# Feed-forward of a two-block transformer: a third quad of weight tiles in seven products, with its late sums made by accumulating DMAs

## The chip, the core and the metric

The kernel runs on one core of a Trainium2 chip, as one launch. The metric is the device time of one execution in microseconds (us), the median of several. The engines that matter here are PE (TensorE, the matrix products), DVE (VectorE), ACT (ScalarE), POOL (GpSimd, which here only issues DMAs) and SP (SyncE, whose queue issues the loads of the weights).

## What is computed

Two transformer blocks over 256 tokens of width 2048 in float32. The part that the change touches is the gate and up projection of the first block's feed-forward, with D = 2048 and D_FF = 5632:

```python
h = rms_norm(x, norm_ffn[l])
x = x + (jax.nn.silu(h @ w_ffn_gate[l]) * (h @ w_ffn_up[l])) @ w_ffn_down[l]
```

## The kernel before, in words

**Tiles.** A weight tile is 128 rows by 512 columns (256 KB). The 256 tokens are two halves j of 128. The kernel works through some 400 chunks of four tiles (1 MB); chunk g lies in slot g % 4 of `raw`, and SP issues its load as soon as the chunk four before it has been read for the last time.

**Splitting.** Each tile goes through PE three times, because both operands are split into a rounded high part and a low part. For each *piece* (mostly two tiles) ACT writes `whi` = high part of `raw` (`piece_hi`, L427), DVE writes `wlo` = `raw` - `whi` (`piece_lo`, L432), and PE runs for each product the three matmuls of `three` (L2610 to L2612): high x high, high x low, low x high, each over 512 columns. `whi` and `wlo` have SPLITS = 4 slots: ACT may start on piece q only when PE is done with piece q - 4 (`wait_ge(mm_done, q - (SPLITS - 1))`).

**The phases.** D_FF is 11 blocks f of 512 columns. Block 0 is phase "ffn", block 10 is "ffz", and the nine blocks f = 1 to 9 (NSUM = 9) are phase "ffs", which the change is about. A block of "ffs" has eight *quads* (`pos` = 0 to 7), one chunk each: two tiles of the gate weight and the two tiles of the up weight at the same rows. A quad is a 2 x 2 product of blocks (two token halves by gate and up, summed over two tiles of rows). Done plainly (`eight_products`) it has eight products, so 24 matmuls, in two pieces of 12. By Strassen's scheme in Winograd's form (`seven_products`) it has seven, so 21 matmuls, in four pieces: n = 0 with 6 matmuls (two raw tiles), n = 1 with 3 (one tile), n = 2 with 6 and n = 3 with 6, the last two on *sums* of weight tiles. Before, positions 3 and 5 are such quads (`SEVEN = {3: 0, 5: 1}`). Of their sums DVE makes all: one addition over two tiles (L438), and then two over one tile each (L440, L442), all between pieces n = 1 and n = 2 (`block_sums`). The sums and differences of the activations (`SH`, `SL`) are made once, in phase "ffn".

**The banks.** A block sums into four of the eight banks of PSUM (`own_banks`), and its seven-product quads also into the other four (`shared_banks`), which are the own banks of the block before. After the last seven-product quad ACT copies one shared bank (`FO`, L1285) and DVE combines them (`fold_shared`, L466 to L471, four operations); PE starts the next block only after that (`wait_ge(fold, ...)`). At `pos` 1 of the next block DVE adds the folded values to the own banks of the block before (`summed`, L1878 to L1881), which frees them; the first seven-product quad of a block waits for this on PE. ACT then does the silu (`silu_summed`, L1253, after `pos` 2), DVE multiplies and transposes (`gated_sum`, L1887 and L1861, after `pos` 2), and 16 small DMAs that SP issues between its weight loads (`turn_block`, at c = 5, 6, 7) turn the block, which is split after `pos` 6 (`gated_hi`, `gated_lo`).

**Order.** Every engine runs one list of instructions written out by hand and waits on semaphores in that order. POOL issues nothing in "ffs".

## Time and profile before

| | |
|---|---|
| median of 3 runs | 2166.47 us (2166.32 to 2166.47) |
| the profiled execution, its own time | 2167.23 us |
| its span in the trace | 2165.5 us |
| busy: PE, DVE, ACT, POOL | 99%, 70%, 50%, 10% of the span |
| mean TensorE clock granted | 0.999 |
| phase "ffs" | nine blocks, from about 419 to 799 us, 42.16 us each |

Times in the rows are us from the start of the span. The own time is 1.7 us longer than the span (start and end of the program), and 0.8 us above the median of the runs.

### The profile page before, as it was taken

How to read it: one execution, taken by the hardware profiler on the slowest of the kernel's cores; microseconds unless marked ns; L12 is line 12 of the kernel's file. 1: busy time of each engine (PE TensorE's matmuls, PEld its weight loads, DVE VectorE, ACT ScalarE, POOL GpSimd, SP SyncE). 2: the span in 40 equal slices, each digit the busy share in tenths (PEclk: the TensorE clock that was granted, in tenths of full speed). 3: DMA queues.
4: the chain of work that ended last, by engine and by line, in shares of the span. 5: the costliest groups of instructions: out<-in, count | busy, mean ns of one | idle time of the engine just before them, and what ended most of it. 6: DMA issues, size and time to landing. Idle time of an engine off the chain costs nothing.

```text
span 2165.5 us, 26086 instructions
## 1 busy us (share of the span) xinstructions
PE 2151.5 (99%) x9865; PEld 1784.5 (82%) x9865; DVE 1513.4 (70%) x1873; ACT 1083.4 (50%) x1355; POOL 219.1 (10%) x376
## 2 busy tenths in 40 slices
PE   9999999999999999999999999999999999999998
PEld 7878888888888888888888888888888888888886
DVE  6676676688888886858566876687766666666546
ACT  6554664455555554535444455445544444444333
POOL 1013024000000001000011361010000000000000
PEclk9999999999999999999999999999999999999999
DMA  9558468667767767667676786766666656765763
GB/s 318 198 176 223 151 227 269 205 189 219 231 187 212 234 213 223 200 221 230 212 230 195 198 229 177 274 225 204 185 205 207 196 187 191 213 186 201 253 202 110
DMA packets 380843, 455.12 MB, mean 210 GB/s; under 512 B 168193, under 2 KB 203409, under 8 KB 379584
## 3 DMA queue, kind: packets, MB, share of 16 engines
q1 hardware_dynamic: 364016, 414.98, 61.4%
q0 software_dynamic: 16432, 38.44, 5.8%
q8 instruction: 68, 1.11, 0.2%
q14 instruction: 39, 0.32, 0.0%
q10 hardware_dynamic: 288, 0.27, 0.0%
HBM read 415.33 MB, written 8.39 MB: 196 GB/s over the span
## 4 chain that ended last, share of the span: by engine, by line
PE 97%; DVE 1%; ACT 1%; DMA 0%; issue 0%; SPq 0%; POOL 0%; ACTq 0%
PE bank L537 21%; PE bank L539 21%; PE bank L538 21%; PE bank L2610 8%; PE bank L2611 8%; PE bank L2612 8%; PE bank L551 1%; PE bank L553 1%; PE bank L552 1%; PE bank L2745 1%; PE bank L2732 1%; PE bank L2442 0%; PE bank L570 0%; DMA mT<-mS 0%; PE bank L2841 0%; PE bank L2842 0%
## 5 line engine op out<-in xcount | busy, mean ns | idle before, releaser
L516 DVE TENSOR_TENSOR wlo<-raw,whi 128x1024 fp32r<-128x1024 f32 (+1 forms) x537 | 643.4, 1213 | 391.4 <-ACT whi L509 389.9
L509 ACT ACTIVATE whi<-raw 128x1024 fp32r<-128x1024 f32 (+1 forms) x537 | 555.7, 1051 | 446.2 <-PE bank L539 418.1
L537 PE MATMUL bank<-whi,T1H 128*128 128x512 f32 (+1 forms) x1524 | 597.3, 392 | 0.0
L539 PE MATMUL bank<-whi,T1L 128*128 128x512 f32 (+1 forms) x1524 | 590.5, 387 | 0.0
L538 PE MATMUL bank<-wlo,T1H 128*128 128x512 f32 (+1 forms) x1524 | 590.1, 387 | 0.0
L427 ACT ACTIVATE whi<-raw 128x1024 fp32r<-128x1024 f32 (+1 forms) x264 | 265.0, 1016 | 268.9 <-PE bank L2612 215.0
L432 DVE TENSOR_TENSOR wlo<-raw,whi 128x1024 fp32r<-128x1024 f32 (+1 forms) x264 | 301.4, 1167 | 96.4 <-ACT whi L427 93.1
L537 PEld LDWEIGHTS bank<-whi,T1H 128*128 128x128 f32 x1524 | 286.3, 188 | 59.3 <-issue 2.3
L539 PEld LDWEIGHTS bank<-whi,T1L 128*128 128x128 f32 x1524 | 286.0, 188 | 59.0
L538 PEld LDWEIGHTS bank<-wlo,T1H 128*128 128x128 f32 x1524 | 286.3, 188 | 56.8
L2610 PE MATMUL bank<-whi,T1H 128*128 128x512 f32 x486 | 189.1, 389 | 0.0
L2611 PE MATMUL bank<-wlo,T1H 128*128 128x512 f32 x486 | 189.1, 389 | 0.0
L2612 PE MATMUL bank<-whi,T1L 128*128 128x512 f32 x486 | 189.1, 389 | 0.0
L2610 PEld LDWEIGHTS bank<-whi,T1H 128*128 128x128 f32 x486 | 91.2, 188 | 19.0
L2612 PEld LDWEIGHTS bank<-whi,T1L 128*128 128x128 f32 x486 | 91.2, 188 | 18.9
L2611 PEld LDWEIGHTS bank<-wlo,T1H 128*128 128x128 f32 x486 | 91.2, 188 | 18.8
L2610 PE MATMUL bank<-whi,T2bH 128*128 128x512 f32 x232 | 90.3, 389 | 0.0
L2611 PE MATMUL bank<-wlo,T2bH 128*128 128x512 f32 x232 | 90.2, 389 | 0.0
L2612 PE MATMUL bank<-whi,T2bL 128*128 128x512 f32 x232 | 90.2, 389 | 0.0
L537 PE MATMUL bank<-whi,T2dH 128*128 128x512 f32 x224 | 87.2, 389 | 0.0
L539 PE MATMUL bank<-whi,T2dL 128*128 128x512 f32 x224 | 87.1, 389 | 0.0
L538 PE MATMUL bank<-wlo,T2dH 128*128 128x512 f32 x224 | 87.1, 389 | 0.0
(471 smaller groups left out, 2603.9 us busy)
## 6 DMA issues: line engine op xcount, KB each, us to landing
raw<-in_ret_w_in SPq DMA_DIRECT2D x64, 1024.0 KB, 5.5
raw<-in_w_ffn_down SPq DMA_DIRECT2D x44, 1024.0 KB, 5.7
raw<-in_attn_w_in SPq DMA_DIRECT2D x40, 1024.0 KB, 5.6
raw<-in_w_in SPq DMA_DIRECT2D x39, 1024.0 KB, 5.4
raw<-in_w_ffn_gate SPq DMA_DIRECT2D x72, 512.0 KB, 3.9
raw<-in_w_ffn_up SPq DMA_DIRECT2D x72, 512.0 KB, 4.9
raw<-in_ret_w_in SPq DMA_DIRECT2D x64, 512.0 KB, 4.7
raw<-in_ret_w_out SPq DMA_DIRECT2D x32, 1024.0 KB, 5.1
```

The source lines that it names most:

```text
L427: eng.activation(whi[:, s, 0:m, :], raw[:, c % RAWS, tiles, :], ACT.Copy).then_inc(hi_ready, 1)
L432: eng.tensor_tensor(wlo[:, s, 0:m, :], raw[:, c % RAWS, tiles, :], whi[:, s, 0:m, :].bitcast(F32), ALU.subtract).then_inc(lo_ready, 1)
L509: eng.activation(hi_[:, s, :, :n], raw[:, c % RAWS, HALF * hf:HALF * (hf + 1), :n], ACT.Copy).then_inc(hi_ready, 1)
L516: eng.tensor_tensor(lo[:, s, :, :n], raw[:, c % RAWS, HALF * hf:HALF * (hf + 1), :n], hi_[:, s, :, :n].bitcast(F32), ALU.subtract).then_in ...
L537: eng.matmul(o, TH[:, kt, xs], hi_[:, s, t, :n], start=first and t == 0, stop=False)
L538: eng.matmul(o, TH[:, kt, xs], lo[:, s, t, :n], start=False, stop=False)
L539: m = eng.matmul(o, TL[:, kt, xs], hi_[:, s, t, :n], start=False, stop=last and t == HALF - 1)
L551: eng.matmul(o, TH[:, kt, xs], hi_[:, s, t, :], start=first and t == 0, stop=False)
L552: eng.matmul(o, TH[:, kt, xs], lo[:, s, t, :], start=False, stop=False)
L2610: mm(o, hi_[xs], whi[:, s, t, :], start=first, stop=False)
L2611: mm(o, hi_[xs], wlo[:, s, t, :], start=False, stop=False)
L2612: return mm(o, lo[xs], whi[:, s, t, :], start=False, stop=last)
```

## The change

Three quads of a block are done in seven products instead of two: `SEVEN = {1: 0, 3: 1, 5: 2}`, in block 9 only positions 1 and 3. In all 26 quads of "ffs" instead of 18.

DVE makes only the first of the sums (`two_sums`, one addition over two tiles, after piece n = 1). The others are made by three accumulating DMAs from tile to tile of `raw`, 256 KB each, which POOL issues: tile 2 += tile 3 once piece n = 0 has been split; then, when this has landed and DVE's sum is there, tile 3 += tile 0 and tile 2 += tile 0. They count on `sums_in`, and ACT's split of piece n = 3 waits for all three.

Piece n = 3 moves: on ACT, DVE and PE it comes after both pieces of the *next* quad (`order`). So the chunk of a seven-product quad stays in use one quad longer, and the loads wait accordingly (`freed`). `summed` stands as before after piece (1, 1), `gated_sum` stands after piece (1, 3); the copy of the shared bank on ACT stands ahead of piece (7, 0); the fold on DVE stands after piece (0, 0) of the next block (`folded`) instead of at the block's end. The differences of the activations are made for three quads instead of two, from a sum of the split parts (`Ax`), one or two pieces later in "ffn".

```diff
@@ -71,8 +71,9 @@
 BY_SP = {"ffn": 0, "down": 11, "ret": 14}
 
 NSUM = 9
-QUADS = [2, 3, 4, 0, 5, 1, 6, 7]
-SEVEN = {3: 0, 5: 1}
+QUADS = [3, 0, 4, 1, 5, 2, 6, 7]
+SEVEN = {1: 0, 3: 1, 5: 2}
+FSEV = len(SEVEN)
 PHASES = [("in1", 44, 1), ("out1", 16, 1), ("ffn", 8, 1), ("ffs", 8 * NSUM, 1), ("ffz", 8, 1), ("down", 44, 1), ("in2", 40, 1),
           ("out2", 16, 1), ("ret", 24, 4), ("out3", 32, 1)]
 
...
@@ -96,12 +97,18 @@
 DOWN = [[4, 5, 6, 7, 8, 9, 0, 10, 1, 11, 2, 12, 3, 13, 14, 15, 16, 17, 18, 19, 20, 21], [4, 5, 6, 0, 7, 1, 8, 2, 9, 3, 10, 11]]
 DQ = [len(DOWN[0]), len(DOWN[0]) + len(DOWN[1])]
 DSEV = 4
-SEVENS = ([PLAN["ffs"][0] + 8 * f + p for f in range(NSUM) for p in SEVEN]
+FFS = [PLAN["ffs"][0] + 8 * f + p for f in range(NSUM) for p in SEVEN if f < NSUM - 1 or p < 5]
+SEVENS = (FFS
           + [PLAN["down"][0] + c for c, k in enumerate(DOWN[0] + DOWN[1]) if k < DSEV])
 
 
 def sevens(g):
     return sum(x < g for x in SEVENS)
+
+
+def freed(g):
+
+    return halves(g + 1) + (2 if g in FFS else 0)
 
 
 def halves(g):
...
@@ -199,9 +206,10 @@
     sg = at("sg", FT, [P, J, W])
     av = at("av", FT + 4 * KB, [P, J, W])
     avT = at("avT", FT + 4 * KB, [P, J, 4, P])
-    SH = at("SH", R0 + 40 * KB, [P, 4, 2, P], F32R)
-    Sf = at("Sf", R0 + 84 * KB, [P, 4, 2, P])
-    SL = at("SL", R0 + 84 * KB, [P, 4, 2, P], F32R)
+    SH = at("SH", R0 + 36 * KB, [P, 4, FSEV, P], F32R)
+    Sf = at("Sf", R0 + 80 * KB, [P, 4, FSEV, P])
+    SL = at("SL", R0 + 80 * KB, [P, 4, FSEV, P], F32R)
+    Ax = at("Ax", R0 + 30 * KB, [P, 2 * FSEV, T])
     FO = at("FO", FT + 8 * KB, [P, 4, W])
     FD = at("FD", FT, [P, 4, W])
     XR = at("XR", FT + 8 * KB, [P, 2, J, W])
...
@@ -399,7 +407,7 @@
         return PLAN[ph][0] + c in SEVENS
 
     def gate_and_up(eng, c, gate, up):
-        eng.wait_ge(lo_ready, halves(PLAN["ffs"][0] + c - RAWS + 1))
+        eng.wait_ge(lo_ready, freed(PLAN["ffs"][0] + c - RAWS))
         seven = is_seven("ffs", c)
         eng.dma_start(raw[:, c % RAWS, 0:4:2, :] if seven else raw[:, c % RAWS, 0:2, :], gate).then_inc(landed[c % RAWS], 16)
         eng.dma_start(raw[:, c % RAWS, 1:4:2, :] if seven else raw[:, c % RAWS, 2:4, :], up).then_inc(landed[c % RAWS], 16)
...
@@ -410,7 +418,8 @@
 
     def piece(ph, c, n):
 
-        q = halves(PLAN[ph][0] + c) + n
+        g = PLAN[ph][0] + c
+        q = halves(g) + n + (2 if g in FFS and n == 3 else -1 if g - 1 in FFS else 0)
         a, z = ((2, 4), (0, 1), (0, 2), (2, 4))[n] if is_seven(ph, c) else (2 * n, 2 * n + 2)
         return q, q % SPLITS, slice(a, z), z - a
 
...
@@ -421,8 +430,10 @@
         q, s, tiles, m = piece(ph, c, n)
         if n == 0:
             land(eng, ph, c, 0)
-        if n >= 2:
-            eng.wait_ge(b_sum, 3 * sevens(PLAN[ph][0] + c) + (1 if n == 2 else 3))
+        if n == 3 and ph == "ffs":
+            eng.wait_ge(sums_in, 48 * sevens(PLAN[ph][0] + c) + 48)
+        elif n >= 2:
+            eng.wait_ge(b_sum, sums_before(PLAN[ph][0] + c) + (1 if n == 2 else 3))
         eng.wait_ge(mm_done, q - (SPLITS - 1))
         eng.activation(whi[:, s, 0:m, :], raw[:, c % RAWS, tiles, :], ACT.Copy).then_inc(hi_ready, 1)
 
...
@@ -431,11 +442,28 @@
         eng.wait_ge(hi_ready, q + 1)
         eng.tensor_tensor(wlo[:, s, 0:m, :], raw[:, c % RAWS, tiles, :], whi[:, s, 0:m, :].bitcast(F32), ALU.subtract).then_inc(lo_ready, 1)
 
-    def block_sums(eng, ph, c):
-
-        n, w = 3 * sevens(PLAN[ph][0] + c), raw[:, c % RAWS, :, :]
+    def sums_before(g):
+        return sum(1 if x in FFS else 3 for x in SEVENS if x < g)
+
+    def order(f):
+
+        late = [p for p in SEVEN if 8 * (f - 1) + p + PLAN["ffs"][0] in FFS]
+        return [(pos, n) for p in range(8) for pos, n in
+                ([(p, n) for n in range(3 if p in late else 2)] + ([(p - 1, 3)] if p - 1 in late else []))]
+
+    def last_seven(f):
+        return max(p for p in SEVEN if 8 * (f - 1) + p + PLAN["ffs"][0] in FFS)
+
+    def two_sums(eng, ph, c):
+
+        w = raw[:, c % RAWS, :, :]
         eng.wait_ge(lo_ready, piece(ph, c, 1)[0] + 1)
         eng.tensor_tensor(w[:, 0:2, :], w[:, 0:2, :], w[:, 1:4:2, :], ALU.add).then_inc(b_sum, 1)
+
+    def block_sums(eng, ph, c):
+
+        n, w = sums_before(PLAN[ph][0] + c), raw[:, c % RAWS, :, :]
+        two_sums(eng, ph, c)
         eng.wait_ge(b_sum, n + 1)
         eng.tensor_tensor(w[:, 3, :], w[:, 0, :], w[:, 3, :], ALU.add).then_inc(b_sum, 1)
         eng.wait_ge(b_sum, n + 2)
...
@@ -923,6 +951,18 @@
                     group_across(pool, line3(sg), line4(avT), r, o_in)
         for n in range(2):
             pool.wait_ge(x1_st[n], 32)
+        for i, g in enumerate(FFS):
+            c = g - PLAN["ffs"][0]
+            w = raw[:, c % RAWS, :, :]
+            pool.wait_ge(lo_ready, piece("ffs", c, 0)[0] + 1)
+            if i:
+                pool.wait_ge(sums_in, 48 * i)
+            pool.dma_start(w[:, 2, :], w[:, 3, :], accum_op=ALU.add).then_inc(sums_in, 16)
+            pool.wait_ge(b_sum, i + 1)
+            pool.wait_ge(sums_in, 48 * i + 16)
+            pool.dma_start(w[:, 3, :], w[:, 0, :], accum_op=ALU.add).then_inc(sums_in, 16)
+            pool.dma_start(w[:, 2, :], w[:, 0, :], accum_op=ALU.add).then_inc(sums_in, 16)
+
         def x2_rows(scr, b):
             return rows(scr)[:, :, b * W:(b + 1) * W]
 
...
@@ -1266,9 +1306,10 @@
             if h == 4:
                 rstd(rstd2, ms1, 3, rs1)
                 table_silu()
-            if h == 6:
-                act.wait_ge(x_parts, 4)
+            if h == 8:
+                act.wait_ge(x_parts, 5)
                 act.wait_ge(x1_st[0], 32)
+                act.wait_ge(x1_st[1], 32)
                 act.activation(SH[:, :, :, :], Sf[:, :, :, :], ACT.Copy).then_inc(x_parts, 1)
             if h == 11:
                 act.wait_ge(x1_st[0], 32)
...
@@ -1276,17 +1317,16 @@
                 block_done(act, "ffn", 3)
                 silu(0)
         for f in range(1, NSUM + 1):
-            for pos in range(8):
-                c = 8 * (f - 1) + pos
-                for n in range(4 if pos in SEVEN else 2):
-                    if pos == 7 and n == 1:
-                        act.wait_ge(mm_done, piece("ffs", c - 2, 3)[0] + 1)
-                        act.wait_ge(acc_out[gate_blk(f - 1) % 2], gate_free(f - 1))
-                        act.activation(FO[:, 0, :], shared_banks(f)[0], ACT.Copy).then_inc(fold, 1)
-                    piece_hi(act, "ffs", c, n)
-                if pos == 2 and f > 1:
+            for pos, n in order(f):
+                if (pos, n) == (7, 0):
+                    act.wait_ge(mm_done, piece("ffs", 8 * (f - 1) + last_seven(f), 1)[0] + 1)
+                    act.wait_ge(acc_out[gate_blk(f - 1) % 2], gate_free(f - 1))
+                    act.wait_ge(acc_out[1 - gate_blk(f - 1) % 2], up_free(f - 1))
+                    act.activation(FO[:, 0, :], shared_banks(f)[0], ACT.Copy).then_inc(fold, 1)
+                piece_hi(act, "ffs", 8 * (f - 1) + pos, n)
+                if (pos, n) == (2, 1) and f > 1:
                     silu_summed(f - 1)
-                if pos == 6:
+                if (pos, n) == (6, 1):
                     gated_hi(f - 1)
         for h in range(16):
             split_hi(act, "ffz", h // 2, h % 2)
...
@@ -1870,6 +1908,10 @@
             dve.sem_inc(ffn_dve, 2)
             turn_gated(f)
 
+        def folded(f):
+            dve.wait_ge(mm_done, piece("ffs", 8 * (f - 1) + last_seven(f), 3)[0] + 1)
+            fold_shared(dve, FO, shared_banks(f), 5 * (f - 1))
+
         def summed(f):
 
             (g0, g1), (u0, u1) = own_banks(f)
...
@@ -1902,29 +1944,40 @@
                 x1_lo(2)
                 for j in range(J):
                     tr_dve(dve, TB["out1"] + j, part(T1H, 3, j), part(T1L, 3, j), k=j)
-            if h == 7:
-                dve.wait_ge(x_parts, 5)
+            if h == 5:
+                dve.wait_ge(x1_st[0], 32)
+                dve.wait_ge(x1_st[1], 32)
+                tt(Ax[:, :, :], T1H[:, 0:2 * FSEV, :].bitcast(F32), T1L[:, 0:2 * FSEV, :].bitcast(F32), ADD).then_inc(x_parts, 1)
+                dve.wait_ge(x_parts, 1)
+                differences(dve, Sf, *(Ax[:, k::2, j * P:(j + 1) * P] for j in range(J) for k in range(2)), x_parts, 1)
+            if h == 8:
+                dve.wait_ge(x_parts, 6)
                 tt(SL[:, :, :, :], Sf[:, :, :, :], SH[:, :, :, :].bitcast(F32), SUB).then_inc(x_parts, 1)
             if h == 9:
                 dve.wait_ge(x1_st[0], 32)
                 dve.wait_ge(x1_st[1], 32)
         for f in range(1, NSUM + 1):
-            for pos in range(8):
+            for pos, n in order(f):
                 c = 8 * (f - 1) + pos
-                lower_parts(dve, "ffs", c)
-                if pos == 1:
+                piece_lo(dve, "ffs", c, n)
+                if n == 1 and is_seven("ffs", c):
+                    two_sums(dve, "ffs", c)
+                if (pos, n) == (0, 0) and f > 1:
+                    folded(f - 1)
+                if (pos, n) == (1, 1):
                     dve.wait_ge(mm_done, halves(PLAN["ffs"][0] + 8 * (f - 1)))
                     if f == 1:
                         gated(0)
                     else:
                         summed(f - 1)
-                if pos == 2 and f > 1:
+                if (pos, n) == (1, 3) and f > 1:
                     gated_sum(f - 1)
-                if pos == 6:
+                if (pos, n) == (6, 1):
                     gated_lo(f - 1)
-            fold_shared(dve, FO, shared_banks(f), 5 * (f - 1))
         for h in range(16):
             split_lo(dve, "ffz", h // 2, h % 2)
+            if h == 0:
+                folded(NSUM)
             if h == 3:
                 dve.wait_ge(mm_done, halves(PLAN["ffz"][0]))
                 summed(NSUM)
...
@@ -2614,15 +2667,13 @@
         def x_of(k, j):
             return (slice(None), k, slice(j * P, (j + 1) * P))
 
-        def eight_products(f, pos):
-            c = 8 * (f - 1) + pos
-            for n in range(2):
-                q, s, _, _ = piece("ffs", c, n)
-                pe.wait_ge(lo_ready, q + 1)
-                for t in range(HALF):
-                    for j in range(J):
-                        m = three(own_banks(f)[n][j], T1H, T1L, x_of(2 * QUADS[pos] + t, j), s, t, pos == 0 and t == 0, pos == 7 and t == 1)
-                m.then_inc(mm_done, 1)
+        def eight_products(f, pos, n):
+            q, s, _, _ = piece("ffs", 8 * (f - 1) + pos, n)
+            pe.wait_ge(lo_ready, q + 1)
+            for t in range(HALF):
+                for j in range(J):
+                    m = three(own_banks(f)[n][j], T1H, T1L, x_of(2 * QUADS[pos] + t, j), s, t, pos == 0 and t == 0, pos == 7 and t == 1)
+            m.then_inc(mm_done, 1)
 
         def eight_of(ph, c, own, TH, TL, k, first, last):
             for n in range(2):
...
@@ -2654,13 +2705,13 @@
                     m = three(m6, DH, DL, D_[2], s, 1, opens, closes)
                 m.then_inc(mm_done, 1)
 
-        def seven_products(f, pos):
+        def seven_products(f, pos, n):
             r = SEVEN[pos]
-            if r == 0:
+            if r == 0 and n == 0:
                 pe.wait_ge(acc_out[gate_blk(f - 1) % 2], gate_free(f - 1))
                 pe.wait_ge(acc_out[1 - gate_blk(f - 1) % 2], up_free(f - 1))
-                pe.wait_ge(x_parts, 6)
-            seven_of("ffs", 8 * (f - 1) + pos, own_banks(f), shared_banks(f), T1H, T1L, SH, SL, QUADS[pos], r, r == 0, r == len(SEVEN) - 1)
+                pe.wait_ge(x_parts, 7)
+            seven_of("ffs", 8 * (f - 1) + pos, own_banks(f), shared_banks(f), T1H, T1L, SH, SL, QUADS[pos], r, r == 0, pos == last_seven(f), (n,))
 
         for h in range(16):
             if h == 0:
...
@@ -2675,11 +2726,11 @@
         for f in range(1, NSUM + 1):
             if f > 1:
                 pe.wait_ge(fold, 5 * (f - 1))
-            for pos in range(8):
-                if pos in SEVEN:
-                    seven_products(f, pos)
+            for pos, n in order(f):
+                if is_seven("ffs", 8 * (f - 1) + pos):
+                    seven_products(f, pos, n)
                 else:
-                    eight_products(f, pos)
+                    eight_products(f, pos, n)
         for h in range(16):
             products(pe, "ffz", h // 2, h % 2, T1H, T1L, 4 * (h % 8 // 2), gate_blk(NF - 1) + h // 8, W, h % 8 == 0, h % 8 == 7)
 
```

The places left out number the semaphores of the later phases anew and declare the new one.

## Rows read from the trace of the kernel before

**Rows 1.** The profile's page: busy time by engine; chain that ended last, by engine.

```profile
PE 2151.5 (99%) x9865; PEld 1784.5 (82%) x9865; DVE 1513.4 (70%) x1873; ACT 1083.4 (50%) x1355; POOL 219.1 (10%) x376
...
PE 97%; DVE 1%; ACT 1%; DMA 0%; issue 0%; SPq 0%; POOL 0%; ACTq 0%
```

**Rows 2.** Windows view: busy us (instructions) per engine, clock, DMA share, GB/s.

```profile
400.00:790.00 390.00, 390.00 (x1722) 323.06 (x1721) 322.39 (x344) 204.15 (x216) 0.00 (x0) 1.00 0.67 207
```

**Rows 3.** Timeline of ACT, blocks 4 to 6: start, duration, engine, line, operation.

```profile
593.48 1.06 ACT L427 ACTIVATE whi<-raw 128x1024 fp32r<-128x1024 f32 x1 [1.60 <-PE bank L2612]
...
598.92 1.06 ACT L427 ACTIVATE whi<-raw 128x1024 fp32r<-128x1024 f32 x1 [1.60 <-PE bank L2612]
599.89 1.32 ACT L1253 ACTIVATE sg<-sg,small 128x512 f32<-128x512 f32 x2
601.70 1.06 ACT L427 ACTIVATE whi<-raw 128x1024 fp32r<-128x1024 f32 x1 [0.49 <-PE bank L2612]
604.36 0.63 ACT L427 ACTIVATE whi<-raw 128x512 fp32r<-128x512 f32 x1 [1.60 <-PE bank L2612]
...
611.22 3.10 ACT L427 ACTIVATE whi<-raw 128x1024 fp32r<-128x1024 f32 x3 [0.30 <-PE bank L2612]
...
617.71 1.06 ACT L427 ACTIVATE whi<-raw 128x1024 fp32r<-128x1024 f32 x1 [2.51 <-DVE raw L438]
...
642.05 1.32 ACT L1253 ACTIVATE sg<-sg,small 128x512 f32<-128x512 f32 x2
```

**Rows 4.** Timeline of PE where a block begins.

```profile
593.06 0.39 PE L2612 MATMUL bank<-whi,T1L 128*128 128x512 f32 x1
593.28 0.39 PE L2610 MATMUL bank<-whi,T1H 128*128 128x512 f32 x1
593.51 0.39 PE L2611 MATMUL bank<-wlo,T1H 128*128 128x512 f32 x1
```

**Rows 5.** Timeline of DVE, from a fold to the first sum of position 3.

```profile
586.04 0.68 DVE L466 TENSOR_TENSOR FO<-bank,FO 128x512 f32<-128x512 f32 x1
...
588.08 0.69 DVE L471 TENSOR_TENSOR FO<-bank,FO 128x512 f32<-128x512 f32 x1
...
594.58 1.23 DVE L432 TENSOR_TENSOR wlo<-raw,whi 128x1024 fp32r<-128x1024 f32 x1 [1.43 <-ACT whi L427]
595.72 0.68 DVE L1878 TENSOR_TENSOR sg<-bank,FO 128x512 f32<-128x512 f32 x1
...
598.11 1.21 DVE L432 TENSOR_TENSOR wlo<-raw,whi 128x1024 fp32r<-128x1024 f32 x1
...
601.25 1.41 DVE L1887 SCALAR_TENSOR_TENSOR av<-av,small,sg 128x512 f32<-128x512 f32 x2
602.58 1.30 DVE L1861 STREAM_TRANSPOSE sg<-av 128x512 f32<-128x512 f32 x2
603.80 1.92 DVE L432 TENSOR_TENSOR wlo<-raw,whi 128x1024 fp32r<-128x1024 f32 x2
605.76 1.23 DVE L438 TENSOR_TENSOR raw<-raw 128x1024 f32<-128x1024 f32 x1
```

**Rows 6.** DMA issues, whole span: count, KB each, median us from issue to landing.

```profile
raw<-in_w_ffn_gate SPq DMA_DIRECT2D x72, 512.0 KB, 3.9
...
raw<-in_w_ffn_up SPq DMA_DIRECT2D x8, 1024.0 KB, 5.6
...
z<-Bh POOLq DMA_DIRECT2D x1, 508.0 KB, 7.2
z<-Bh POOLq DMA_DIRECT2D x1, 504.0 KB, 10.2
...
rs__163<-in_rope_s POOLq DMA_DIRECT2D x1, 256.0 KB, 2.9
...
rc<-in_rope_c POOLq DMA_DIRECT2D x1, 256.0 KB, 5.8
```

**Rows 7.** Issue of one 256 KB DMA by POOL (one line's view).

```profile
L986 POOL DMA_DIRECT2D dpos<-in_dist x1: 552/552/552, 1421.7 to 1421.7; - x1
```

More of the change, by code:

```diff
@@ L338, in two_blocks @@
     gF_in, ffn_dve, ffn_act = (sem(x) for x in ("gF_in", "ffn_dve", "ffn_act"))
-    x_parts, b_sum, fold = (sem(x) for x in ("x_parts", "b_sum", "fold"))
+    x_parts, b_sum, sums_in, fold = (sem(x) for x in ("x_parts", "b_sum", "sums_in", "fold"))
     xr1_in, x1_st, xr3_in, xr4_in = ([sem(f"{x}{n}") for n in range(2)] for x in ("xr1_in", "x1_st", "xr3_in", "xr4_in"))
@@ L391, in load @@
             if g >= RAWS:
-                eng.wait_ge(lo_ready, halves(g - RAWS + 1))
+                eng.wait_ge(lo_ready, freed(g - RAWS))
         else:
@@ L1320, in _ @@
             if c == 4:
-                act.wait_ge(x_parts, 11)
+                act.wait_ge(x_parts, 12)
                 act.activation(SHd[:, :, :, :], Sfd[:, :, :, :], ACT.Copy).then_inc(x_parts, 1)
@@ L1833, in x1_lo @@
             turned_lo(dve, SQ["out1"] + b, T1H[:, cols_, :], T1L[:, cols_, :], avT)
-            if b == 0:
-                differences(dve, Sf, *(avT[:, j, k:4:2, :] for j in range(J) for k in range(2)), x_parts, 0)
         for b in range(FB):
@@ L1969, in _ @@
                 tt(Af[:, :, :], T2bH[:, 0:2 * DSEV, :].bitcast(F32), T2bL[:, 0:2 * DSEV, :].bitcast(F32), ADD).then_inc(x_parts, 1)
-                dve.wait_ge(x_parts, 7)
-                differences(dve, Sfd, *(Af[:, k::2, j * P:(j + 1) * P] for j in range(J) for k in range(2)), x_parts, 7)
+                dve.wait_ge(x_parts, 8)
+                differences(dve, Sfd, *(Af[:, k::2, j * P:(j + 1) * P] for j in range(J) for k in range(2)), x_parts, 8)
             if c == 5:
-                dve.wait_ge(x_parts, 12)
+                dve.wait_ge(x_parts, 13)
                 tt(SLd[:, :, :, :], Sfd[:, :, :, :], SHd[:, :, :, :].bitcast(F32), SUB).then_inc(x_parts, 1)
@@ L2634, in eight_of, with seven_of @@
                 m.then_inc(mm_done, 1)
-        def seven_of(ph, c, own, shared, TH, TL, DH, DL, k, r, opens, closes):
+        def seven_of(ph, c, own, shared, TH, TL, DH, DL, k, r, opens, closes, ns=range(4)):
             (g0, g1), (u0, _) = own
@@ L2640, in seven_of @@
             D_ = [(slice(None), n, r, slice(None)) for n in range(4)]
-            for n in range(4):
+            for n in ns:
                 q, s, _, _ = piece(ph, c, n)
@@ L2705, in _ @@
                         pe.wait_ge(acc_out[1 - gate_blk(NF - 1) % 2], up_free(NF - 1))
-                        pe.wait_ge(x_parts, 13)
+                        pe.wait_ge(x_parts, 14)
                     if k == 0 and sb == 1:
```

## Prediction

> **What bounds the kernel now.** The page says it first: PE is busy 99% of the span and makes 97% of the chain that ended last [rows 1]. In the windows view of the phase that the change touches PE is busy for the whole 390 us, at full clock; DVE is busy 322 of them (83%), ACT 204, the DMA engines 67% [rows 2]. So every matmul taken away is worth its time, and every wait put into PE's list costs its time: nothing absorbs it.
>
> How near is such a wait? ACT's timeline shows the silu of one block at 599.89 and of the next at 642.05 [rows 3]: a block takes 42.16 us. It has 6 x 24 + 2 x 21 = 186 matmuls, so one takes 0.2267 us, with no idle between. The split of a piece starts when PE is done with the piece four before: the last matmul of a block starts at 593.06 and lasts 0.39, the next block starts at 593.28 [rows 4], and ACT goes on at 593.48 [rows 3], 0.20 after it. I call the start of PE's block T and write times from it. ACT and DVE are thus three pieces ahead of PE at most, and only while these are big: three pieces of a seven-product quad (6 + 3 + 6 matmuls) last 3.4 us, while a split takes 1.06 on ACT and 1.23 on DVE. ACT was already held up 2.51 us by DVE's sums, at 617.71, without PE noticing [rows 3].
>
> **What is removed.** Eight more quads with 3 matmuls less: 24 x 0.2267 = 5.4 us, 0.68 in each of blocks 1 to 8, none in block 9. On DVE two additions over one tile go in 18 quads, and one over two tiles and two splits come in 8; its total hardly moves, its order does.
>
> **The order on DVE.** In the new list the first seven-product quad is position 1 and the second position 3, with piece (1, 3) and `gated_sum` right ahead of (3, 0). I follow it without any delay by a DMA. Piece (1, 0) has left PE at 30 x 0.2267 = 6.8, so the split (2, 1) runs on ACT from 7.0 to 8.0, then the silu (1.32 alone, 1.25 ahead of the next) to 9.25 [rows 3], then the split (1, 3) to 10.3. DVE splits it until 11.5 (1.14 from start to start [rows 5]). `gated_sum` takes 2.55 (601.25 to 603.80 [rows 5]): 14.05. Splits (3, 0) and (3, 1) take 1.92, the sum 1.23, each with its 0.04 of wait [rows 5]: 17.2. Only now may ACT split (3, 2), 1.06, and DVE, 1.23: 19.55, and about 0.2 until PE runs. PE wants this piece after 12+12+6+3+6+12+12+6+6+3 = 78 matmuls, at 17.7. It waits 2.0 us. Before, `gated_sum` stood after position 2 with no seven-product quad behind it until DVE was four to five us ahead. Blocks 2 to 9 have this wait: 8 x 2.0 = 16 us.
>
> `summed` also comes nearer: PE's piece (1, 0) wants it at T + 5.44. DVE starts the split (1, 1) at about T + 0.9, the sum over two tiles at 1.6, `summed` at 2.75, and ends 2.4 later (595.72 to 598.11 [rows 5]), at 5.2: in time by 0.1 to 0.2, or late by 0.1 to 0.6 if DVE is behind; I price it inside the chain below. The fold moves behind (0, 0), four operations from 586.04 to 588.77, 2.7 us [rows 5]; PE needs it at T. The split (0, 0) may start at T - 6.6, so it ends before T - 4, the fold at about T - 1.5: covered, and with DVE 2 us behind no longer.
>
> **The accumulating DMAs.** No row shows one. Call L the time from POOL's first issue for a quad to the landing of the third DMA: the first must land (L1), then two are issued, 0.55 each [rows 7], and land (L2). From below: a plain 256 KB load by POOL with little beside it takes 2.9 [rows 6]; 0.55 more for the pair gives 2.9 + 3.45 = 6.4. From above: another such load took 5.8, and the two 500 KB copies from tile to tile that POOL issued together took 7.2 and 10.2 [rows 6]; 5.8 + 7.2 = 13.0. Between them I take the bytes: an accumulate reads two tiles and writes one, so I price one as 512 KB, like the half chunks of this phase that land in 3.9, and two as 1 MB, 5.6 [rows 6]: L = 9.5. These rows were read under the load under which the new DMAs will run: they are issued 1 to 2 us after SP's loads, because the same piece frees both.
>
> For the one term that decides, two pages of the Trainium skill disagree. "DMA: Bandwidth & Descriptors", section "Anatomy of one DMA", gives about 2.0 us and the bytes at 436 GB/s for a DMA of POOL; by it L would be an estimated 2.6 + 3.8 = 6.4, and the DMAs would be hidden. No run here shows it for an accumulating one. "Collectives: The Full Stack", section "The bandwidth ceiling", says that an add in the DMA engines needs two source reads on one ring and so goes at half the rate of a copy; by it L is nearer to the upper half.
>
> **The chain they make.** ACT's list is in order, so the split (p, 3), which waits for the landing, holds the split (p+2, 0), and only when DVE has done that may POOL start the next quad's first DMA. From T: the splits (0, 0), the fold and (0, 1), (1, 0) let POOL start at T + 1.6. Landing at 1.6 + L. Then the splits (1, 3), `gated_sum` and (3, 0): 6.15 (1.06 + 1.23, 2.55, 1.23, with 0.1 of waits). L again. Then two splits on ACT (2.05) and one on DVE with waits: 3.6. L again. Then (5, 3) through ACT, DVE and to PE 2.55, its 6 matmuls 1.36, quad 7 5.45 and 0.15 of waits: 9.5. A block so takes at least 3L + 20.9. With L = 9.5 that is 49.5, against 42.16. The chain overtakes the other bound (42.16 - 0.68 + 2.0 + 0.1 = 43.6) at L = 7.6; beyond it each us of L costs 3 us a block.
>
> **Sum.** Blocks 2 to 8: 7 x 7.4 = 52. Block 1, without `gated_sum`: 47.5, so 5.4. Block 9, two such quads: 48.0, so 5.8. Together 63 us. The work in "ffn" (a sum and larger differences, some 4 us on DVE, where it is about 2.5 us ahead of PE at worst and idles over 1 us a piece) I put at nothing; its cover gone, it costs under 1 us once. The loads of weights that are issued one quad later have 2 quads (10 us) for a landing of 5.6: hidden, except that of position 1 of the next block, which lands just as ACT wants it and costs what it is late. The profiled execution then takes 2167.2 + 63 = 2230; the median is 0.8 below it: 2229.5.
>
> **The rivals.**
> (A) As told: the chain of landings sets the pace, L between 7.6 and 12: 2177 to 2292, likeliest 2229.5. For it: the row of 3.9 at this very load. Chance 0.60.
> (B) The landings are hidden, L below 7.6: only the wait at (3, 2) stays, 16 - 5.4 = 11 us more: 2177. For it: the 2.9 of a 256 KB load, and the first page of the skill. Against it: 256 KB rows up to 5.8. Chance 0.16.
> (C) The accumulates are as slow as the copies from tile to tile: L = 13, a block 60 us: 15.9 + 7 x 17.9 + 12.9 = 154 more, 2320. For it: two reads each, 2.4 MB more a block beside 8.4 MB of loads, on DMA engines that are at 67%. Against it: the bursts leave gaps. Chance 0.19.
> (D) Faster: the order on DVE costs nothing, and the landings are hidden. One mechanism would do it: DVE ends (3, 1) and its sum at least 2.0 us earlier than I work out, at 15.2 instead of 17.2. Then 5.4 us are won: 2161. Against it: each term is a row, and the same reckoning gives the split times of before to 0.1 us. Chance 0.03.
> (E) A wait at (3, 2) of half the size gives back what is won: 2167. Chance 0.02.
>
> **The numbers.** Under 0.2% (4.3 us) the measurement of this kernel can't tell from no change. Slower: A, B and C, 0.95; same 0.02; faster 0.03. The range reaches from B, 2177, over A to its upper end, 2295; it leaves out C, D and E, where nearly all of C lies above it.
>
> **What would show it.** PE idle ahead of the pieces (3, 2), (3, 3), (5, 2) and (5, 3) of each block, about 7 to 8 us a block in sum, and a silu every 49 to 50 us; ACT's wait for a POOL DMA as the longest wait of the phase; the three DMAs of a quad landing 9 to 10 us after the first issue. If the landings take under 7.6, only one idle time of 2 us a block, released by DVE, is left (B). The prediction is wrong in kind if PE is not idle at (3, 2) with DVE's sum ending at T + 17, and wrong in size by 3 us a block for each us of L.

## The result: 134 us slower, beyond the upper end of the range

The changed kernel takes 2300.65 us (median of 4 runs, 2298.22 to 2303.42), the kernel before 2166.46 us beside it: the ratio is 1.0619, 95% interval 1.0607 to 1.0632. The forecast was 2229.5 us, with a range to 2295. The direction and the mechanism were right; the size was off by a factor of two, and one term carries nearly all of it.

The page of the changed kernel, busy time by engine, PEclk and DMA in slices, the chain that ended last, and two groups of instructions. Against [rows 1]:

```profile
PE 2186.7 (95%) x9841; PEld 1796.3 (78%) x9841; DVE 1516.2 (66%) x1862; ACT 1091.2 (47%) x1371; POOL 285.1 (12%) x454
...
PE   9999999987777878999999999999999999999998
...
PE 78%; DMA 13%; DVE 5%; issue 2%; ACT 2%; POOL 1%; SPq 0%; POOLq 0%; ACTq 0%
PE bank L565 20%; PE bank L567 20%; PE bank L566 20%; DMA raw<-raw 12%; DVE wlo L443 3%; PE bank L2663 3%; PE bank L2664 3%; PE bank L2665 3%; ACT whi L438 1%; PE bank L579 1%; PE bank L581 1%; PE bank L580 1%; POOL raw L963 1%; PE bank L2796 1%; PE bank L2783 1%
...
L2663 PE MATMUL bank<-whi,T1H 128*128 128x512 f32 x446 | 184.9, 415 | 74.9 <-DVE wlo L443 74.9
```

The 24 matmuls are gone (9865 to 9841), nearly all the time lost lies in slices 9 to 16 of the 40 (from 460 to 919 us), which are "ffs", and the chain that ended last now has 12% of the span in the DMAs from `raw` to `raw`.

The windows view of two blocks of the changed kernel, against [rows 2]:

```profile
597.00:655.40 58.40, 46.15 (x185) 36.17 (x184) 36.47 (x38) 23.57 (x26) 7.68 (x9) 0.91 0.72 191
655.40:714.00 58.60, 47.21 (x189) 37.33 (x188) 36.98 (x40) 24.20 (x27) 8.56 (x10) 0.91 0.74 202
```

PE is busy 46 of 58 us, and the clock granted to it falls to 0.91. A block takes 58.1 us (the silus of ACT's timeline at 488.25 and 895.05 us are 406.80 us and 7 blocks apart) instead of 42.16 [rows 3]. Where PE stands, from its timeline in one of these blocks (the bracket is the idle time ahead of the matmul):

```profile
613.98 0.50 PE L2663 MATMUL bank<-whi,T1H 128*128 128x512 f32 x1 [1.26 <-DVE wlo L443]
618.19 0.50 PE L2663 MATMUL bank<-whi,SH 128*128 128x512 f32 x1 [1.85 <-DVE wlo L443]
628.14 0.50 PE L2663 MATMUL bank<-whi,T1H 128*128 128x512 f32 x1 [1.22 <-DVE wlo L443]
633.49 0.50 PE L2663 MATMUL bank<-whi,SH 128*128 128x512 f32 x1 [1.61 <-DVE wlo L443]
646.94 0.80 PE L2663 MATMUL bank<-whi,T1H 128*128 128x512 f32 x1 [6.32 <-DVE wlo L443]
```

These are the pieces (3, 0), (3, 2), (3, 3), (5, 2) and (5, 3), 12.3 us of idle time. All are put down to DVE's splits. The chain says what DVE itself waited for. The chain of this block in order of time (start, duration, what; short links left out):

```profile
597.04 5.55 DMA raw<-raw
...
603.12 0.54 POOL raw L963
603.66 4.28 DMA raw<-raw
...
607.96 1.07 ACT whi L438
...
610.19 1.41 DVE av L1929 x2
611.60 1.21 DVE sg L1899 x2
612.82 1.12 DVE wlo L443
...
614.22 3.74 DMA raw<-raw
...
618.49 0.54 POOL raw L963
619.02 6.72 DMA raw<-raw
...
629.51 5.36 DMA raw<-raw
...
635.40 0.54 POOL raw L963
635.94 8.61 DMA raw<-raw
...
650.58 0.61 DVE FO L494
...
655.79 5.42 DMA raw<-raw
```

Read it as the forecast's formula, 3L + 20.9. From the first issue of a quad to its last landing it shows L = 10.9 (597.04 to 607.94), 11.5 (614.22 to 625.74) and 15.0 (629.51 to 644.55), together 37.4. Between them lie 6.3 us (two splits and `gated_sum`), 3.8 us (two splits), and 11.2 us (the splits of (5, 3) and of what follows, the fold), together 21.3, where 20.9 was worked out. No matmul stands in it: for these blocks PE is not the bound at all. That is not quite the path of the forecast, which had 6.8 us of matmuls (those of (5, 3) and quad 7) behind quad 5's landing. The chain has ACT's copy, five splits and the fold on DVE there. 11.2 us against the 11.1 worked out is a match of the number, not of the path.

### The profile page after: what moved, and what is told of

The parts are those of the page before. It is cut to its first block, busy times and chain, and to the rows that moved or that the text cites. A ratio compares the mean times of both kernels' runs of the same rounds, so it can differ in the third digit from the quotient of the medians.

```text
span 2297.4 us, 26198 instructions
## 1 busy us (share of the span) xinstructions
PE 2186.7 (95%) x9841; PEld 1796.3 (78%) x9841; DVE 1516.2 (66%) x1862; ACT 1091.2 (47%) x1371; POOL 285.1 (12%) x454
## 4 chain that ended last, share of the span: by engine, by line
PE 78%; DMA 13%; DVE 5%; issue 2%; ACT 2%; POOL 1%; SPq 0%; POOLq 0%; ACTq 0%
PE bank L565 20%; PE bank L567 20%; PE bank L566 20%; DMA raw<-raw 12%; DVE wlo L443 3%; PE bank L2663 3%; PE bank L2664 3%; PE bank L2665 3%; ACT whi L438 1%; PE bank L579 1%; PE bank L581 1%; PE bank L580 1%; POOL raw L963 1%; PE bank L2796 1%; PE bank L2783 1%
## 5 line engine op out<-in xcount | busy, mean ns | idle before, releaser
L544 DVE TENSOR_TENSOR wlo<-raw,whi 128x1024 fp32r<-128x1024 f32 (+1 forms) x537 | 643.3, 1213 | 383.7 <-ACT whi L537 382.1
L443 DVE TENSOR_TENSOR wlo<-raw,whi 128x1024 fp32r<-128x1024 f32 (+1 forms) x280 | 314.1, 1154 | 206.9 <-ACT whi L438 205.3
L2664 PE MATMUL bank<-wlo,T1H 128*128 128x512 f32 x446 | 180.9, 406 | 0.0
L2665 PE MATMUL bank<-whi,T1L 128*128 128x512 f32 x446 | 179.6, 403 | 0.0
L619 POOL DMA_DIRECT2D rTs<-rb x64 | 37.1, 586 | 468.6 <-DVE rb L2333 462.5
```

Source lines behind the costliest of these rows:

```text
L443: eng.tensor_tensor(wlo[:, s, 0:m, :], raw[:, c % RAWS, tiles, :], whi[:, s, 0:m, :].bitcast(F32), ALU.subtract).then_inc(lo_ready, 1)
L544: eng.tensor_tensor(lo[:, s, :, :n], raw[:, c % RAWS, HALF * hf:HALF * (hf + 1), :n], hi_[:, s, :, :n].bitcast(F32), ALU.subtract).then_in ...
L619: eng.dma_start(dst[:, :, r, :], src[:, :, b, :]).then_inc(landed_, 16)
L2664: mm(o, hi_[xs], wlo[:, s, t, :], start=False, stop=False)
L2665: return mm(o, lo[xs], whi[:, s, t, :], start=False, stop=last)
```

## The experiments

All times are medians beside runs of the kernel before on the same chip; the ratio is to those. A block is timed by the distance of silus in the trace, a mean over seven or eight blocks where nothing else is said. L is a mean over the 9, 9 and 8 quads at the three positions, from POOL's issue times and the landings of the three DMAs.

| run | us | ratio (95%) |
|---|---|---|
| nobody waits for the DMAs | 2179.52 | 1.0059 (1.0042 to 1.0076) |
| kernel before plus the DMAs | 2166.37 | 0.9999 (0.9990 to 1.0009) |
| copies in place of adds | 2250.42 | 1.0387 (1.0370 to 1.0405) |
| `gated_sum` later | 2287.97 | 1.0562 (1.0545 to 1.0580) |
| late sums by DVE | 2178.96 | 1.0054 (1.0038 to 1.0071) |
| the same, `gated_sum` later | 2187.06 | 1.0090 (1.0073 to 1.0107) |
| nobody waits, small loads | 2176.57 | 1.0043 (1.0027 to 1.0059) |
| one landing a quad | 2229.70 | 1.0290 (1.0275 to 1.0306) |
| two quads | 2259.23 | 1.0426 (1.0410 to 1.0442) |
| turned sooner | 2312.95 | 1.0667 (1.0651 to 1.0683) |
| three quads in place | 2162.08 and 2162.12 | 0.9978 (0.9969 to 0.9988) and 0.9982 (0.9973 to 0.9991) |

### Is it the waiting or the traffic?

In the first kernel the three DMAs of a quad are of the same size and kind, but read `T1H` and add into two tiles that nothing else uses, so nothing waits for them; the two late sums of `raw` are left out. The second puts the same three DMAs into the kernel before.

```diff
-            pool.dma_start(w[:, 2, :], w[:, 3, :], accum_op=ALU.add).then_inc(sums_in, 16)
+            pool.dma_start(spA[:, :], T1H[:, 0:2, :].bitcast(F32).rearrange("p a b -> p (a b)"), accum_op=ALU.add).then_inc(sums_in, 16)
...
-            eng.wait_ge(sums_in, 48 * sevens(PLAN[ph][0] + c) + 48)
+            pass
```

> The changed kernel, but its three accumulating DMAs a quad go to two spare tiles (source: a tile of activations) and nobody in the feed-forward waits for them; piece n = 3 is split from tiles that lack the two late sums, so those sums are left out of the result. Theory 1 (the landings, one after the other, set the pace): the chain is gone, only DVE's order stays, a wait of 2.0 us ahead of piece (3, 2): 43.6 us a block, 2177 us in all (2172 to 2185). Rival 2 (the DMAs' traffic delays the weight loads, so that PE waits for weights): the traffic is the same, so the time stays within 20 us of the 2301 of the changed kernel.

> The kernel before (two seven-product quads, all sums by DVE), to which POOL adds the same 78 accumulating DMAs of 256 KB, at the same places of the stream, into spare tiles; nobody in the feed-forward waits for them. Theory 1: 2166.5 us, within 2 us: their traffic alone costs nothing. Rival 2 (traffic): each block slower by several us, 2200 us or more.

The first took 2179.52 us and the second 2166.37, as the theory of the landings had it. In the first the landings are as long as in the changed kernel (L is 12.9, 11.7 and 11.3), only nobody waits for them. In the second the traffic is all there. The windows view of the kernel before with the DMAs added:

```profile
420.00:600.00 180.00, 180.00 (x796) 149.05 (x795) 150.71 (x161) 94.38 (x100) 31.81 (x38) 1.00 0.95 259
```

The DMA engines are at 95% instead of 67% [rows 2] and PE does not stop once. The gate half of a chunk then lands after 6.0 us instead of 3.9 [rows 6], and the four slots of `raw` absorb it. So this traffic costs the kernel before nothing, and 121 of the 134 us (2300.65 - 2179.52) are the wait for the landings. What is left, 13 us over before, is mostly DVE's order: in the first run PE's only long stop in the block shown is

```profile
615.65 0.50 PE L2670 MATMUL bank<-whi,SH 128*128 128x512 f32 x1 [1.57 <-DVE wlo L445]
```

at (3, 2), and this block takes 43.4 us (43.6 worked out). The mean of the first seven is 43.9. With small weight loads, further down, the first seven all take 43.4 and the kernel takes 3 us less, so some 3 of the 13 us come with the full loads.

### How much of a landing is what?

```diff
-            pool.dma_start(w[:, 2, :], w[:, 3, :], accum_op=ALU.add).then_inc(sums_in, 16)
+            pool.dma_start(w[:, 2, :], w[:, 3, :]).then_inc(sums_in, 16)
...
```

The other two lose their `accum_op` in the same way, so that blocks are copied and not added.

> The changed kernel with its three DMAs a quad as plain copies (same tiles, same waits, same bytes written, no addition, so the two late sums are not sums). Theory 1 with the price by bytes read (an add reads two tiles, a copy one): the sum of landings of a quad falls from 12.5 us to about 9.5, a block to 3 x 9.5 + 20.9 = 49.4 us, 2229 us in all (2210 to 2245). Rival 3 (the landing is set by the fixed part and by the weight loads ahead in the same DMA engines, not by the addition): within 10 us of 2301.

2250.42 us, between the two, so both expectations fell. The block takes 52.0 us, and its three L are 8.9, 9.2 and 12.3, against 10.9, 10.8 and 14.8: an add costs 1.6 to 2.5 us a quad more than a copy. It isn't POOL's time between two issues. One line of each kernel, changed and with copies:

```profile
L963 POOL DMA_DIRECT2D raw<-raw x26: 839/844/851, 428.5 to 909.2; - x26
```

```profile
L963 POOL DMA_DIRECT2D raw<-raw x26: 539/539/557, 428.4 to 859.5; - x26
```

POOL's record of an add lasts 0.84 us against 0.54, and that of the third (L964) 1.18 against 0.54. But the third is issued 0.54 us after the second in both kernels, and the second 0.6 us after the first has landed in both. The 2 us lie between issue and landing. With no weight load beside them, the pair of quad 1 lands after 3.3 and 4.3 us as adds and after 2.3 and 2.6 as copies (medians). So the addition explains 2 of 12.2 us.

On top of the kernel in which nobody waits, the weight loads of "ffs" bring an eighth of each block (gate shown, up alike):

```diff
-        eng.dma_start(raw[:, c % RAWS, 0:4:2, :] if seven else raw[:, c % RAWS, 0:2, :], gate).then_inc(landed[c % RAWS], 16)
+        eng.dma_start(raw[:, c % RAWS, 0:4:2, 0:64] if seven else raw[:, c % RAWS, 0:2, 0:64], gate[:, :, 0:64]).then_inc(landed[c % RAWS], 16)
...
```

> The run in which nobody waits for the DMAs, with the weight loads of the nine blocks cut to 64 of 512 columns (the rest of each tile is left as it stands, so the products are of other numbers). It is made to read the landings of the accumulating DMAs with little beside them. If the weight loads lengthen them: 3.5 us or less for the first, 4.5 or less for the last of a quad, against 4.5 to 5.7 with full loads. If the addition sets them: unchanged within 0.5 us. The time of the kernel stays within 5 us of 2179.5.

The landings, last line of a view of one issue line, first with small loads, then with full ones (least, median, most), for the first DMA of a quad:

```profile
L966 POOL DMA_DIRECT2D spA<-T1H x26: 832/846/949, 425.3 to 784.8; - x26
...
DMA to landing us min/median/max: 3.2/3.5/3.7
```

```profile
L966 POOL DMA_DIRECT2D spA<-T1H x26: 832/846/949, 425.0 to 788.1; - x26
...
DMA to landing us min/median/max: 3.4/4.5/7.6
```

The third's median is 4.7 against 5.7, 0.2 more than expected; the first's 3.5 and the time of the kernel (2176.57 us) came out as expected. A quad's L is 8.9, 9.6 and 9.6, nearly equal, against 12.9, 11.7 and 11.3. So an add with little beside it lands after 3.5 us, and the weight loads add 1.6 to 4.0 us a quad and nearly all of the spread. L = 9.5, the forecast's term, is what the DMAs take with hardly a load beside them. The page "DMA: Bandwidth & Descriptors" of the Trainium skill, section "Anatomy of one DMA", gives an estimated 2.6 us for these bytes and says nothing of adds; the copies of quad 1 show 2.3 to 2.6, the adds 3.3 and more. The page "Collectives: The Full Stack" of the Trainium skill, section "The bandwidth ceiling", has a reduce-scatter between cores, whose adds read two sources, at half the rate of an all-gather, which copies; in whole landings here a quad's adds take 12.2 us against 10.1 for copies, and no run shows the transfer by itself.

```diff
-            for r in {5: (0,), 6: (1,), 7: (2, 3)}.get(c, ()):
+            for r in {5: (0, 1), 6: (2, 3)}.get(c, ()):
```

> The changed kernel with the 16 small DMAs that turn a block issued eight at c = 5 and eight at c = 6 instead of four, four and eight at c = 5, 6 and 7, so that none is issued beside the pair of quad 5, which lands after 8.6 us where those of quads 1 and 3 take 4.3 and 6.7. If they lengthen it: quad 5's landings fall from 15.0 towards 12 us and quad 3's grow by less, 8 to 16 us won in all (2285 to 2293). If the weight loads beside it do: within 4 us of 2301.

2312.95 us, 12 more than the changed kernel: both expectations on the total fell. The three L are 10.9, 13.4 and 13.2: quad 5 lost 1.6 us, quad 3 gained 2.6. 1.0 us more a block in sum fits 12 us in all (3L for nine blocks: 9). It does not follow that the small DMAs lengthen what they run beside, because the edit moved more than them. SP issues them and the weight loads in one list, eight small ones take it 5 to 8 us, and the chunk behind them comes later. From SP's timeline, first in the changed kernel, then here:

```profile
629.04 6.38 SPq L619 DMA_DIRECT2D avT<-sg  x8
635.47 0.60 SPq L412 DMA_DIRECT2D raw<-in_w_ffn_gate  x1
```

```profile
615.59 5.44 SPq L619 DMA_DIRECT2D avT<-sg  x8
621.08 0.60 SPq L412 DMA_DIRECT2D raw<-in_w_ffn_gate  x1
```

POOL issues the pair of quad 5 at 635.40 in the changed kernel and the pair of quad 3 at 621.14 here, each with a whole chunk of weights in the same microsecond. They are the slowest pairs of their kernels. Sorted by what runs beside the pair, its last landing (median) is:

| pair | beside it | us |
|---|---|---|
| quad 1, changed kernel | nothing | 4.3 |
| quad 5, turned sooner | nothing | 4.3 |
| quad 3, `gated_sum` later | 4 small DMAs, the end of a chunk | 4.7 |
| quad 3, changed kernel | 4 small DMAs, more of a chunk | 5.8 |
| quad 5, changed kernel | a whole chunk, mostly 3 small DMAs about to land | 8.5 |
| quad 3, turned sooner | a whole chunk, 10 or 11 small DMAs | 8.5 |

With the same chunk beside it, eight more small DMAs change nothing. So by these rows it is the weight load that lengthens the pair, and the small DMAs push that load onto it. This was read from the traces after the runs; no run moved the chunk alone.

### Are the landings in series, and is `gated_sum` in the chain?

Here DVE makes the first sum itself, after piece n = 0, and a quad waits for one landing less:

```diff
-            pool.wait_ge(lo_ready, piece("ffs", c, 0)[0] + 1)
...
-            pool.dma_start(w[:, 2, :], w[:, 3, :], accum_op=ALU.add).then_inc(sums_in, 16)
...
+                    tt(raw[:, c % RAWS, 2, :], raw[:, c % RAWS, 2, :], raw[:, c % RAWS, 3, :], ADD).then_inc(b_sum, 1)
```

> The changed kernel with one landing a quad instead of two, one after the other: DVE makes tile 2 += tile 3 itself (one addition over one tile, after piece n = 0), and POOL issues only the pair tile 3 += tile 0 and tile 2 += tile 0, once DVE's sum over two tiles is there. Theory 1 (landings in series): from the time of POOL's old first issue it now takes 0.7 for the added addition, 2.0 for piece n = 1 and the sum, and 7.0 for the pair, 9.7 us against 12.5: 3 x 9.7 + 20.9 = 50.0 us a block, 2230 us in all (2215 to 2245). Rival 5 (only the last landing counts, the first is hidden behind DVE's work): within 10 us of 2301, or slower by DVE's added 18 us.

2229.70 us: the first DMA was in the chain, and taking it out is worth 71 us although DVE has more to do. Rival 5 fell. That 2230 was expected is luck, though. The pair lands 6.2 us after its first issue in the mean, not 7.0, and three landings in series are no longer what the block waits for. Its chain from one pair of quad 3 to the next (links left out):

```profile
593.58 6.65 DMA raw<-raw
600.25 1.07 ACT whi L438
...
607.43 0.61 SPq L619
608.08 4.92 DMA avT<-sg
...
616.53 0.50 PE bank L2663
...
643.72 6.22 DMA raw<-raw
```

One pair stands in it, then SP's list with eight of the small DMAs that turn a block, the landing of the last of them, the split of the turned block, and PE. From 480 to 840 us the chain has 14% in the DMAs of `raw` (58% in the changed kernel), 18% in the turning (its landings and SP's issues) and 24% in PE. The path over the turning of the block happens to take 50.0 us too.

```diff
-                if (pos, n) == (1, 3) and f > 1:
+                if (pos, n) == (3, 2) and f > 1:
                     gated_sum(f - 1)
```

> The changed kernel with DVE's gated_sum after piece (3, 2) instead of after (1, 3). Theory 1: its 2.55 us stand in the chain between the landing of quad 1's sums and POOL's first DMA for quad 3; without them a block is 2.55 us shorter (58.4 to 55.9), 8 blocks: 2280 us (2276 to 2284). Rival 4 (the wait at (3, 2) is not in one chain with the landings, or the later turning of the block costs as much): within 5 us of 2301.

2287.97 us: 12.7 us faster, not 20, and outside the expected 2276 to 2284. The block falls from 58.1 to 56.5. POOL's first issue for quad 3 does come sooner (14.6 us after quad 1's, 593.37 to 607.94, instead of 17.2), but the L of quad 5 rose from 14.8 to 15.4: its first DMA lands after 6.7 us in the mean instead of 5.4. The turning DMAs moved with `gated_sum`, and SP's chunk behind them came nearer to it; whether that is the reason was not tried. The three L are 0.5 us more in sum; another 0.4 of the 2.55 stays open. The rival (no gain) fell.

In the next two DVE makes all the late sums, after piece (p + 1, 0), and there are no such DMAs; the second also has `gated_sum` at (3, 2):

```diff
...
+                    tt(v[:, 3, :], v[:, 0, :], v[:, 3, :], ADD).then_inc(sums_in, 1)
+                    dve.wait_ge(sums_in, 2 * k + 1)
+                    tt(v[:, 2, :], v[:, 3, :], v[:, 2, :], ADD).then_inc(sums_in, 1)
```

> The changed kernel without its accumulating DMAs: DVE makes the two late sums itself (two additions over one tile) after piece n = 0 of the next quad; order, deferral and three quads as in the change. Theory 1: no landing is left, only DVE's order: waits of 2.0 us at (3, 2) and some 0.4 to 0.6 at (1, 0) and (5, 3); 44.75 us a block, 2187 us in all (2180 to 2194). A rival that blames the deferral of piece n = 3 itself, or the third quad, for most of the loss expects 2250 or more.

> As the run with DVE's own late sums, and gated_sum after piece (3, 2) instead of (1, 3). Theory 1: where no landing sets the pace there is nothing to shorten, and the 2.55 us only move from (3, 2) to (4, 0), where they cost as much or more: 2187 to 2196 us, not faster than that run by more than 1 us. A rival that takes the gain of the same move in the changed kernel for a gain of the place as such expects 12 us less than that run.

2178.96 us, 1 us below the expected 2180 to 2194: the block takes 43.6 us, 1.1 less than reckoned; of the waits only that at (3, 2) shows (1.75 us in seven blocks, 1.57 in the eighth). The rival that blames the deferral or the third quad for most of the loss fell. With `gated_sum` later it took 2187.06, 8.1 us more, while the same move made the changed kernel 12.7 us faster. The two together show that the move pays by the chain of landings and not by the place as such.

### Two quads, and the clock

```diff
-QUADS = [3, 0, 4, 1, 5, 2, 6, 7]
-SEVEN = {1: 0, 3: 1, 5: 2}
+QUADS = [2, 3, 4, 0, 5, 1, 6, 7]
+SEVEN = {3: 0, 5: 1}
...
-                if (pos, n) == (1, 3) and f > 1:
+                if (pos, n) == (2, 1) and f > 1:
                     gated_sum(f - 1)
```

> The DMA sums and the deferral of piece n = 3 at the two quads of the kernel before (positions 3 and 5; gated_sum after position 2, as before). Theory 1: a block has one landing chain from quad 3 to quad 5 (12.3 us and then about 14) and the rest of the block, five plain quads, to catch up in: 48.6 us a block, 2218 us in all (2200 to 2245). Rival 6 (each such quad costs a fixed 134 / 26 = 5.2 us): 18 x 5.2 = 93 more than before, 2259 us.

2259.23 us: my theory missed by 41 us, and the rival's number came out to the microsecond. The trace shows in part why. The block takes 52.6 us, with L = 10.5 and 14.9, where 12.3 and about 14 were put in: 0.9 us less in sum. What I did not put in stands in the chain of the block:

```profile
612.28 8.46 DMA raw<-raw
620.77 1.06 ACT whi L438
621.86 1.24 DVE wlo L443
623.14 0.80 PE bank L2663
623.93 0.43 PE bank L2664
624.36 0.43 PE bank L2665
...
628.20 0.43 PE bank L2665
628.63 0.27 PE bank L2663
628.89 0.23 PE bank L2664
```

After a stop of 6.20 us PE's matmuls come every 0.43 us instead of every 0.227: the granted clock is at 1.2 instead of 2.4 GHz for 5.5 us after the stop, which costs 12 matmuls some 0.2 us each. After the nine long stops of this phase it is 6 to 13 matmuls, 9.7 in the mean, 2.0 us a block. With only two such quads PE stands in the chain between one block's last landing and the next block's first, so all that slows PE there is paid. The block is 4.0 us longer than the 48.6 of my theory although the landings are 0.9 shorter, so the rest of it is 4.9 longer. The clock has 2.0 of that; 2.9 stays open. In the changed kernel the same happens, but there, in the blocks looked at, the chain passes through ACT, DVE and POOL. A fixed cost per quad is not refuted by this run; it falls by the others, in which 26 such quads cost 134, 84, 63, 121 or 146 us more, as their landings and the place of `gated_sum` change. That 18 quads cost as much each as 26 is then a coincidence of two sums. This account of the clock was read from the trace after the run; no run took the clock alone away.

### A version that beats both

The three quads of the scheme stand at 2, 4 and 6, their sums and products are made in place by DVE (`block_sums`, as the kernel before has it), there are no DMAs for them, `summed` comes after (1, 0) and `gated_sum` at (2, 0). Both runs are of this kernel:

```diff
-QUADS = [3, 0, 4, 1, 5, 2, 6, 7]
-SEVEN = {1: 0, 3: 1, 5: 2}
+QUADS = [3, 4, 0, 5, 1, 6, 2, 7]
+SEVEN = {2: 0, 4: 1, 6: 2}
...
-                    two_sums(dve, "ffs", c)
+                    block_sums(dve, "ffs", c)
...
-                if (pos, n) == (1, 1):
+                if (pos, n) == (1, 0):
...
-                if (pos, n) == (1, 3) and f > 1:
+                if (pos, n) == (2, 0) and f > 1:
                     gated_sum(f - 1)
```

> Three seven-product quads at positions 2, 4 and 6 (2 and 4 in block 9), all sums by DVE at once and piece n = 3 in its place as in the kernel before, no DMAs; summed after piece (1, 0) and silu and gated_sum after (2, 0), so that DVE has its long work behind it before the first such quad. By the same reckoning 41.66 us a block against 42.16: 8 x 0.5 = 4 us won, 2162.5 us (2160 to 2168). If DVE at three such quads a block has too little left whatever its order: 2170 or more.

> The same kernel as the run with three quads in place and all sums by DVE, timed in five rounds: 2162 us, 4 to 5 us less than before, with an interval that excludes no change.

2162.08 and 2162.12 us, 4.6 and 4.4 us (0.2%) under the kernel before, with both intervals below 1; the slowest of the 21 runs (2163.86) lies below the fastest of the kernel before (2165.81). The windows view and two silus (ACT's timeline) of it:

```profile
600.00:780.00 180.00, 180.00 (x793) 148.17 (x792) 173.81 (x190) 104.48 (x113) 0.00 (x0) 1.00 0.69 212
```

```profile
594.10 1.32 ACT L1278 ACTIVATE sg<-sg,small 128x512 f32<-128x512 f32 x2
635.70 1.32 ACT L1278 ACTIVATE sg<-sg,small 128x512 f32<-128x512 f32 x2
```

A block takes 41.60 us. DVE is busy 97% of this stretch (94% of the 180 us before it) and PE does not wait: DVE had room for the third quad after all, once its long work (`summed`, `gated_sum`) came ahead of the first such quad. Of the gain of 24 matmuls, 5.4 us, 4.5 is there.

## Why the prediction was right in kind and wrong in size

- **The bound and the gain.** PE was the bound, a matmul 0.2267 us. Right: with order and sums in a good place the gain is 4.5 of 5.4 us.
- **DVE's order.** A wait of 2.0 us at (3, 2) in eight blocks. Right: where no landing is waited for it is 1.57 and 1.75 us, and the two kernels without a wait for a DMA lie 12 to 13 us above before, where 11 was worked out for it (2177); the one with small weight loads lies 10 above. (The changed kernel's 1.85 us stand behind a late landing.) The small waits ahead of (1, 0) didn't show.
- **The chain.** At least 3L + 20.9 us a block. Right for the changed kernel: 37.4 + 21.3 in the chain of one block; with the mean L (36.5) 57.4 against 58.1 measured. Its last part matched by luck: 6.8 us of matmuls were put there, and DVE's splits and fold stand there. In the run with copies 30.4 + 20.9 = 51.3 against 52.0 is in part luck too, since PE has 13% of its chain (4% in the changed kernel) and some blocks leave one of the three quads out.
- **L, the term that failed: "L = 9.5".** It is 10.9, 10.8 and 14.8, in the mean 12.2. The step that failed is "I price one as 512 KB, like the half chunks of this phase that land in 3.9, and two as 1 MB, 5.6". The first landed after 4.9 in the mean (5.4, 3.9, 5.5), 1.0 more. Then POOL took 0.56 to issue the next, which had been put at nothing. The pair landed 6.7 after its first issue: 0.55, and 6.1 for the last (4.4, 5.8, 8.2), 1.1 more. With 12.2 in place of 9.5 the same sum gives 57.5 for blocks 2 to 8, 55.6 for block 1 and 53.4 for block 9: 107 + 14 + 11 = 132 us more, 2299 against 2300.65.
- **Why L failed.** The forecast held that its rows were "read under the load under which the new DMAs will run". They were not: with an eighth of the weight loads L is 9.4, so 9.5 is the price nearly without load. And the pair of quad 5, which SP's next chunk of weights meets in the same microsecond, lands after 8.5 us where one with nothing beside it takes 4.3. That an add is dearer than a copy (2 us a quad) the forecast had allowed for, by twice the bytes. The row of 3.9, besides, is that of the gate halves alone. The up halves, of the same size and issued 0.4 us behind them, land after 4.9, by the page of the kernel before:

```profile
raw<-in_w_ffn_up SPq DMA_DIRECT2D x72, 512.0 KB, 4.9
```

- **The weight loads, put at nothing.** Nearly right for what they cost PE: nothing is lost in the kernel before with the same traffic, and some 3 us in the changed one with nobody waiting. What they cost the landings is in L.
- **The clock.** Not in the forecast. The changed kernel's chain doesn't pass through it in the blocks shown; in the kernel with two quads it costs 2.0 us a block.
- **The rivals.** B (hidden) fell at L above 7.6. C, the accumulates as slow as copies from tile to tile, had L = 13 and 2320 us: its price was nearer (2301) than that of A. Of its reasons the load on the DMA engines held. The rows of 7.2 and 10.2 us did not: copies of 256 KB in the same places took 2.6 to 6.3 (medians of the last of a pair), less than the adds. A's stretch to 2292 ended 9 us below the result.

## What to carry to other kernels

Work that is moved off a busy engine onto DMAs is paid in latency: ask what is queued behind the wait for the landing, and whether the next DMA is released from behind that same wait. If it is, the landings add up, here 3 x 12.2 us in a block that took 42 before. Price a landing not by the median of its like but beside what the same event releases, and look at what else waits in the list of the engine that issues the big loads; read the chain of a run that hit its forecast too, for one here hit it by another path; and before work is handed away, try the order on the busy engine, for here it alone won what the DMAs were to win.
